# Squares of the second norm added on GpSimd, operations of GpSimd counted one by one, and more buffers for the value pages

## The reference

```python
sh1, sc1, g1, sh2, sc2, g2 = _modulation(c, w_mod, b_mod)
h = _rmsnorm(x, norm1_w) * (1 + sc1) + sh1
z = h @ w_in
rq, rk, rv, rg, mq, mk, mv = jnp.split(z, SPLITS, axis=-1)
ret_out, ret_s = _retention_branch(...)        # rotary on rq and rk, decayed scan in chunks of 128
moba_out = moba_mix(...)                       # prompt: causal; sample: top 3 blocks of the cache + own tokens
x = x + g1 * (jnp.concatenate([ret_out, moba_out], axis=-1) @ w_out)
h2 = _rmsnorm(x, norm2_w) * (1 + sc2) + sh2    # the second norm: mean of x*x over the 1024 features
x = x + g2 * ((jax.nn.silu(h2 @ w_gate) * (h2 @ w_up)) @ w_down)
```

## Time and profile before

| what | value |
|---|---|
| median of 3 runs | 1039.15 us (1037.05 to 1048.32) |
| the profiled execution | 1034.07 us, its span 1032.2 us |
| PE busy | 961.6 us, 93% |
| DVE busy | 624.5 us, 60% |
| ACT busy | 338.4 us, 33% |
| POOL busy | 139.4 us, 14% |
| chain that ended last | PE 72%, DVE 8%, DMA 7%, issue 5%, SP's queue 4%, DVE's queue 2% |
| bytes moved | 269.14 MB, mean 261 GB/s |

### The profile page before, as it was taken

How to read it: one execution, slowest core, us unless ns; L and a number is a source line. 1 busy time by engine, 2 the same in 40 slices (tenths; PEclk the granted TensorE clock), 3 DMA queues, 4 the chain that set the end, 5 groups by cost and what they waited for, 6 DMA issues and landing times.

```text
span 1032.2 us, 20974 instructions
## 1 busy us (share of the span) xinstructions
PE 961.6 (93%) x7919; PEld 675.8 (65%) x7919; DVE 624.5 (60%) x1067; ACT 338.4 (33%) x735; POOL 139.4 (14%) x129
## 2 busy tenths in 40 slices
PE   3879998999999987979989999999999999999996
PEld 2557775766666644547756767676777777777775
DVE  1566874677767667876788584432655555453244
ACT  5412233334333624542252152332333222121113
POOL 0011111444210132204151220000000000000000
PEclk9899999999999989999989899999999999999998
DMA  9978877999786889988998668778476988787652
GB/s 340 364 257 282 284 252 268 296 274 300 255 287 215 276 320 390 356 288 280 362 320 285 231 230 265 230 228 267 144 218 167 240 226 231 218 251 248 204 194 87
DMA packets 217973, 269.14 MB, mean 261 GB/s; under 512 B 13473, under 2 KB 168425, under 8 KB 209682
## 3 DMA queue, kind: packets, MB, share of 16 engines
q1 hardware_dynamic: 110226, 126.65, 38.7%
q10 hardware_dynamic: 98432, 74.04, 23.6%
q0 software_dynamic: 9216, 67.11, 17.7%
HBM read 260.04 MB, written 5.64 MB: 257 GB/s over the span
## 4 chain that ended last, share of the span: by engine, by line
PE 72%; DVE 8%; DMA 7%; issue 5%; SPq 4%; DVEq 2%; ACT 1%; POOLq 1%; POOL 1%; ACTq 0%
PE banks L1128 13%; PE banks L1129 12%; PE banks L1130 12%; PE banks L1078 6%; PE banks L1216 4%; PE banks L1141 4%; PE banks L1143 4%; PE banks L1142 4%; PE banks L1161 4%; DVE KT L1846 3%; DMA V<-in_cache_v 3%; DMA K<-in_cache_k,kidx 1%; SPq L420 1%; PE banks L1340 1%; DMA early<-in_w_mod 1%
## 5 line engine op out<-in xcount | busy, mean ns | idle before, releaser
L658 ACT ACTIVATE whi<-raw 128x1024 fp32r<-128x1024 f32 (+1 forms) x76 | 78.6, 1035 | 298.0 <-PE banks L1130 144.4
L1128 PE MATMUL banks<-ahi,whi 128*128 128x512 f32 x416 | 169.2, 407 | 0.1
L1846 DVE STREAM_TRANSPOSE KT<-K 128x2048 f32<-128x2048 f32 x63 | 145.5, 2310 | 30.0 <-DMA K<-in_cache_k,kidx 15.1
L1129 PE MATMUL banks<-alo,whi 128*128 128x512 f32 x416 | 163.5, 393 | 0.0
L1130 PE MATMUL banks<-ahi,rawlo 128*128 128x512 f32 x416 | 163.3, 393 | 0.0
L1809 DVE TENSOR_TENSOR rawlo<-raw,whi 128x1024 fp32r<-128x1024 f32 (+1 forms) x76 | 91.3, 1201 | 54.3 <-ACT whi L658 51.2
L523 POOL DMA_INDIRECT K<-in_cache_k,kidx x64 | 64.0, 1000 | 412.4 <-DVE KT L1846 363.7
L1128 PEld LDWEIGHTS banks<-ahi,whi 128*128 128x128 f32 x416 | 78.7, 189 | 31.2 <-issue 13.1
L1141 PE MATMUL banks<-ahi,whi 128*128 128x512 f32 x216 | 90.2, 417 | 1.2 <-DVE rawlo L1816 0.9
L1130 PEld LDWEIGHTS banks<-ahi,rawlo 128*128 128x128 f32 x416 | 78.8, 189 | 17.3
L1161 PE MATMUL banks<-KT,qbd 128*32 128x128 f32 x2048 | 74.0, 283 | 15.7 <-DVE KT L1846 13.0
(11 more groups left out here) (330 smaller groups left out, 1462.1 us busy)
## 6 DMA issues: line engine op xcount, KB each, us to landing
V<-in_cache_v SPq DMA_DIRECT2D x184, 256.0 KB
rawm<-in_w_mod ACTq DMA_DIRECT2D x14, 1024.0 KB
raw<-in_w_in ACTq DMA_DIRECT2D x12, 1024.0 KB
zT<-in_cache_v SPq DMA_DIRECT2D x48, 256.0 KB
raw<-in_w_gate ACTq DMA_DIRECT2D x22, 512.0 KB
raw<-in_w_up ACTq DMA_DIRECT2D x22, 512.0 KB
srw<-in_w_gate SPq DMA_DIRECT2D x22, 512.0 KB, 5.6
srw<-in_w_up SPq DMA_DIRECT2D x22, 512.0 KB, 7.3
```

The source lines that it names most:

```text
L658: act.activation(whi[t % 2][:, 0:kd, :], raw[u][:, 0:kd, t % 2 * P:(t % 2 + 1) * P], ACT.Copy).then_inc(s_hi, 1)
L1128: pe.matmul(out[:, :], whi[t % 2][:, k, :], hi(k), start=(first and n == 0), stop=False)
L1129: pe.matmul(out[:, :], whi[t % 2][:, k, :], lo(k), start=False, stop=False)
L1846: dve.transpose(KTb[:, :, :, :], Kb[g % 2][:, :]).then_inc(s_kt, 1)
```

## The change

1. Value groups 1 and 3 get four tiles of their own (`zT` from `RQ`, which the projection fills only later), so SP loads group 1 right behind group 0. Group 2 then waits for group 0's pages, group 4 for group 2's.
2. From group 17 to group 28 the values rotate through three rings in place of two (`raw[1]`, then `scr` and `free`, then `V`), with four more semaphores. Each group waits for the pages of the group three before it. ACT starts the first `w_out` chunk into `raw[1]` after group 26 in place of group 25.
3. The squares of the second norm: ACT writes the first into `rb`, and POOL adds those of k = 1 to 6 to it, one after each key gather from group 47 to group 52. PE sums `rb` and the last square alone, 2 sums in place of 8.
4. In `rotate` and `rotate_half` the drains go. Each operation raises `s_srot` or `s_rk`, and POOL waits for that count.

```diff
+RING_2 = {g: (1, 5)[(g - 17) % 3] for g in range(17, 28) if (g - 17) % 3 < 2}
+RING_FROM = min(RING_2)
+RING_2.update({1: 6, 3: 6})
+RING_2.update({g: 2 if g < 32 else 3 if g < 53 else 4 for g in range(29, NG, 2)})
+LANE = lambda g: 0 if g not in RING_2 else 2 if RING_2[g] == 5 else 1
...
     def values_before(g):
-        return max((x for x in range(g) if (x in RING_2) == (g in RING_2)), default=None)
+        return max((x for x in range(g) if LANE(x) == LANE(g)), default=None)
...
-            if g == 27:
+            if g == 18:
                 sp.wait_ge(s_md, NMOD)
...
-            pool.tensor_tensor(other, other, C("sin"), ALU.mult)
-            pool.tensor_tensor(z, z, C("cos"), ALU.mult)
-            pool.drain()
-            pool.tensor_tensor(z, z, other, ALU.add)
-            pool.drain().then_inc(s_rk, 1)
+            pool.tensor_tensor(other, other, C("sin"), ALU.mult).then_inc(s_srot, 1)
+            pool.tensor_tensor(z, z, C("cos"), ALU.mult).then_inc(s_srot, 1)
+            pool.wait_ge(s_srot, 2 * (m - M_TURN + 1))
+            pool.tensor_tensor(z, z, other, ALU.add).then_inc(s_rk, 1)
...
+        def add_squares(k):
+            pool.wait_ge(s_sqx, k + 1)
+            if k > 1:
+                pool.wait_ge(s_sqa, k - 1)
+            pool.tensor_tensor(rb[:, :], rb[:, :], stage[k % 2][:, :], ALU.add).then_inc(s_sqa, 1)
...
+            if 1 <= g - R_OUT - 3 < KT - 1:
+                add_squares(g - R_OUT - 3)
...
-                if f >= 3:
-                    act.wait_ge(s_ssm, f - 2)
-                act.activation(stage[(f - 1) % 2][:, :], x2T[:, f - 1, :], ACT.Square).then_inc(s_sqx, 1)
+                if f >= 4:
+                    act.wait_ge(s_sqa, f - 3)
+                act.activation(rb[:, :] if f == 1 else stage[(f - 1) % 2][:, :], x2T[:, f - 1, :], ACT.Square).then_inc(s_sqx, 1)
...
+        def sum_squares():
+            pe.matmul(DB[:, 0:TT], ident, C("pad0")[:, 0:TT], start=True, stop=False, skip_group_check=True)
+            pe.wait_ge(s_sqa, KT - 2)
+            sum_over_features(rb, False)
+            pe.wait_ge(s_sqx, KT)
+            sum_over_features(stage[1], True).then_inc(s_ssm, 1)
...
-            if f:
-                sum_squares(f - 1)
             if f == KT - 1:
                 turn_probs(B_NORM, 0)
-                sum_squares(KT - 1)
+                sum_squares()
```

More of the change, by code:

```diff
@@ L261, in decoder_step @@
              [at(B["K"] + ROWS * W + W * i, f"V{4 + i}", [P, W]) for i in range(4)],
-             [scr[:, 0, :], scr[:, 1, :], free[:, 0, :], free[:, 1, :]]]
+             [scr[:, 0, :], scr[:, 1, :], free[:, 0, :], free[:, 1, :]],
+             [zT[:, RQ + i, :] for i in range(4)]]
     ffa = at(ZT, "ffa", [P, 10, 2, T], F32R)
@@ L342, in decoder_step @@
     s_k = [sem(f"k_loaded{i}") for i in range(2)]
-    s_v = [sem(f"v_loaded{i}") for i in range(8)]
+    s_v = [sem(f"v_loaded{i}") for i in range(12)]
     s_kt, s_lg, s_own, s_s1 = sem("k_turned"), sem("logits"), sem("own_logits"), sem("block_sums")
@@ L384, in values @@
     def values(g):
-        if g in RING_2:
-            return rings[RING_2[g]], s_v[4:8], sum(x <= g for x in RING_2)
-        return rings[0], s_v[0:4], g + 1 - sum(x <= g for x in RING_2)
+        n = LANE(g)
+        return rings[RING_2.get(g, 0)], s_v[4 * n:4 * n + 4], sum(LANE(x) == n for x in range(g + 1))
     def values_before(g):
-        return max((x for x in range(g) if (x in RING_2) == (g in RING_2)), default=None)
+        return max((x for x in range(g) if LANE(x) == LANE(g)), default=None)
     def w_buffer(c):
@@ L451, in _ @@
         sp.wait_ge(s_lg, 9)
-        for s in range(4):
-            page(VB[s], s, s_v[s])
-        for g in range(1, M_TURN + 2 * HP - LAG + 2):
+        for g in range(M_TURN + 2 * HP - LAG + 2):
             m = g + LAG - 2
@@ L457, in _ @@
                 swap_halves(m)
+            bufs, sems, _ = values(g)
             for s in range(4):
-                sp.wait_ge(s_vd, g * 4 + s - 3)
-                page(VB[s], g * 4 + s, s_v[s])
-        with sp.Fori(M_TURN + 2 * HP - LAG + 2, min(RING_2)) as i:
+                if values_before(g) is not None:
+                    sp.wait_ge(s_vd, 4 * values_before(g) + s + 1)
+                page(bufs[s], 4 * g + s, sems[s])
+        with sp.Fori(M_TURN + 2 * HP - LAG + 2, RING_FROM) as i:
             for s in range(4):
@@ L464, in _ @@
                 page(VB[s], i * 4 + s, s_v[s])
-        for g in range(min(RING_2), NG):
+        for g in range(RING_FROM, NG):
             bufs, sems, _ = values(g)
@@ L531, in rotate_half @@
             o = (qrs, krs)[n][:, :].rearrange("p (h c d) -> p h c d", h=H, c=2)
-            pool.tensor_tensor(ta, z[:, :, half, :], cos, ALU.mult)
-            pool.tensor_tensor(tb, z[:, :, 1 - half, :], sin, ALU.mult)
-            pool.drain()
-            pool.tensor_tensor(o[:, :, half, :], ta, tb, op)
-            pool.drain()
+            done = 4 * HP + 3 * (2 * n + half)
+            pool.wait_ge(s_srot, done)
+            pool.tensor_tensor(ta, z[:, :, half, :], cos, ALU.mult).then_inc(s_srot, 1)
+            pool.tensor_tensor(tb, z[:, :, 1 - half, :], sin, ALU.mult).then_inc(s_srot, 1)
+            pool.wait_ge(s_srot, done + 2)
+            pool.tensor_tensor(o[:, :, half, :], ta, tb, op).then_inc(s_srot, 1)
         def masked_k(b):
@@ L723, in keep_z @@
             act.wait_ge(s_ft, m + 3)
+            if Z_OF[m] == RQ:
+                act.wait_ge(s_vd, 4 * 4)
             if Z_OF[m] in (RV, RV + 1):
@@ L874, in _ @@
             if hp == 3:
[L875 removed]
+                act.wait_ge(s_vd, 4 * 27)
                 next_chunk(0)
```

29 lines of the change are left out of this document (11 added, 18 removed).

## The result

| | before | changed |
|---|---|---|
| median of the runs | 1040.59 us (20 runs) | 1034.57 us (20 runs) |
| lowest to highest | 1034.26 to 1049.24 | 1031.14 to 1041.83 |
| the profiled execution | 1034.07 | 1035.24 (span 1033.4) |

The changed kernel takes 0.995 of the time of the kernel before, 95% interval 0.9929 to 0.997. That is 5.2 us less (3.1 to 7.4). The forecast was 11.5 us less. 1034.57 lies inside the wide range of the prediction (1018 to 1037) and outside the forecast's own (1023 to 1033). The two profiled executions don't show the gain, since the one of before was among the fastest of its kernel. So I compare them slot by slot. A slot's start is the first of its key matmuls in PE's timeline (L1161 before, L1180 after), and a slot's length runs to the next slot's start.

The account below looks back on a forecast made before the run. PE, busy 93% of the span, was taken as the bound, its stops as the target. Terms 3.9 + 2.8 + 4.6 + 0.2 = 11.5 us took 1039.15 to 1027.7 us; own range 1023 to 1033, wide range 1018 to 1037.

Parts of the forecast that it names:

- C: Second norm's squares: six PE sums of 0.87 us go, slot 49 loses some; 4.6 us gained if keys come in time.
- D: Drains in POOL's rotations replaced by counts: next key gather leaves 9 us earlier; 0.2 us gained, and C made whole.
- as long as ACT keeps pace: POOL's wait for a square ahead of the next gather costs nothing on this condition, each square being ready early enough.
- no 7.86 on POOL: Expected sign: the 7.86 us drain wait behind a gather in slot 45 disappears, the later gather leaving some 9 us earlier.
- a fallen clock: Sign of being wrong: granted clock falls in a stretch where PE now waits for DVE in one long piece.
- Term A: Slot 13, group 1's own buffer: its value stop goes, 4.94 us becoming 1.04; 3.9 us gained, from 1.3 to 3.9.
- Term B: Three rings in the retention: group 24's 3.7 us stop goes, DVE lets 2.8 us through; bounds 0 and 10.9.
- the third rival: Group 18's stop grows as group 1's shrinks, one more page 1.9 us; 1.2 us gained in all, 1038; chance 0.07.
- a change of this stop by more than 1 us: Sign of being wrong: group 18's stop in the retention, forecast to shorten by 0 to 0.8, changing either way.
- held-by-bytes rival: Bytes limit the retention, output-projection keys stay late: A whole, B zero, C and D 1.1; 5.0 us gained, 1034.2; chance 0.30.
- starved keys: Rival: key gathers land late, 12 slots losing 1.8 us each; net 10 us slower, 1049; chance 0.04.
- The rule on DVE and GpSimd: Two-input DVE instructions contend with GpSimd's SBUF reads: each add could hold DVE 1.28 us; sum 1.3 smaller, 1029 us.

Follow-up runs that it names:

- e3: Kernel before with only the squares added on POOL and counts in place of drains; rings and buffers as before: 1047.55 us, ratio 1.004.
- e5: Kernel before with only the squares added on POOL, all drains kept: 1044.26 us, ratio 1.0017.
- e6: Kernel before with only counts in place of drains, PE still summing the squares: 1040.33 us, ratio 0.9985.
- e4: Changed kernel with the retention state load moved from f = 2 to f = 4, behind the last w_out chunk: 1031.2 us, ratio 0.9884 to the kernel before.
- e8: Changed kernel with the retention state load moved from f = 2 to f = 6, behind all w_out chunks: 1028.08 us, ratio 0.986 to the kernel before.
- e9: Kernel before with only the retention state load moved from f = 2 to f = 6: 1038.81 us, ratio 0.9983.
- e10: Changed kernel without the squares part, PE summing each square as before: 1030.62 us, ratio 0.99 to the kernel before.
- e2: Kernel before with only the three rings for value groups 17 to 28: 1040.91 us, ratio 0.9983.
- e11: Changed kernel without the squares part and with the state load at f = 6: 1028.56 us, ratio 0.9886 to the kernel before.
- e7: Kernel before with squares on POOL, counts for drains and the state load at f = 6: 1042.02 us, ratio 1.0007.
- e12: Changed kernel with two rings in the retention as before and the state load at f = 6: 1030.98 us, ratio 0.9898 to the kernel before.

## Why the prediction was wrong, step by step

**The step that failed is terms C and D, in the sentence that D makes C whole and costs nothing as long as ACT keeps pace.** They were put at 4.8 us of gain and measured at 4.2 us of loss (e3). In the chain of keys the mechanism was right at every place named. The gather leaves 13 us earlier where 9 were forecast; no 7.86 on POOL; slots 43 to 47 are 4.5 us shorter. e5 shows what the prediction said of C without D. What it left out is the other transfer that a slot needs. Each slot takes 1 MB of keys, 1 MB of values and half a 1 MB chunk of w_out, 2.6 MB. At slot 47's 8.42 us in e6 that is 311 GB/s, at the 7.66 of the changed kernel 342, and the transfer engines gave 377, 313, 362, 401, 407 and 338 in the six stretches from 470 to 500. Those full stretches held the state load as well. The drain had been a throttle: it kept back gathers while the state load was under way and until just before the last chunk was issued (share 0.59 at 485 to 490 before, 1.03 now). I had asked who waits for the keys, and never who else uses the engines once the keys come early. ACT doesn't keep pace, since it waits for the chunk on its own queue.

The runs show three things about this. The chunk's lateness makes the stop, through ACT's split and DVE's part of it (the chain through the chunk, and slot 48 with the chunk's time in the table). Its place behind the state load matters: with that order changed the chunk comes 5 to 6 us sooner and the kernel is 7 to 9 us faster (e4, e8), while the same move gives the old kernel 1.8 (e9). And neither C nor D alone makes the stop in full: both together do (e5, e6, e10 against e3 and the changed kernel). That it takes both because a shorter slot asks more of full engines is the likeliest reading, from the numbers above, but no run varied the bytes of a slot at a fixed length, and none issued the chunk earlier or from another queue, so it is argued and not shown. Two readings limit it. Full engines alone don't make the chunk late: before, they were as full behind its issue (shares 1.05 and 1.02 from 490 to 500), and it took 8.5 us at most. And its place in the queue doesn't give the size: the state load landed 5.6 us ahead of the chunk's issue before, and 0.7 (e5), 2.2 (e10), 2.7 (e3) and 4.0 us (the changed kernel) behind it, and the chunk took 8.0, 11.3, 17.6 and 17.2 in these four. So 4.0 of the 17.2 us passed before the state load had landed, and what held the chunk for the other 13.2 stays open. The Trainium skill (DMA: Bandwidth & Descriptors, Queues, rings and completion order) says that each DMA engine goes round the queues that have work. By it ACT's queue keeps a third of the engines against SP's and the gathers', an estimated 7.7 us for 1 MB at a third of 407 GB/s, and the chunk shares that third with the state load while both are under way. The runs agree in kind, since the chunk took 10.9 us in e8 without the state load and 17.2 behind it in the changed kernel, but not in size: even the 10.9 is more than an equal third gives. No run here shows the shares of the queues by themselves.

**The price of the stop** was 6.95 us in slot 48 and 1.3 in slot 49 against the old profile, and by slot 54 the changed kernel was 1.5 us behind the old one's profile. Part of that price is the clock, 0.50 at 505 to 510. The prediction had a fallen clock among the things that would make it wrong, but with no place or price.

**Term A** (3.9, from 1.3 to 3.9) was right for the profiled execution: 24.69 to 20.81 is 3.9. Against the runs it was mis-sized: 8.5 (6.0 to 11.1) measured. Six other profiles without part A have a mean of 28.6 us in slots 13 and 14, so 7.7 are gained there. The term was taken from the one profile, and I carried the profile's 5 us under the median over unchanged, without asking in which places a slower execution is slower. This was one of them. No run shows a cost of the early megabyte, as forecast.

**Term B** (2.8, bounds 0 and 10.9) agrees with the 1.8 of e2, whose interval (-0.7 to 4.3) also holds no gain at all. In slots 29 to 42 the eight profiles with two rings have a mean of 98.4 us, the six with three rings 94.9, 3.5 less. Group 24 came on time as forecast. Group 18's stop, which I left as it was, grew instead: slot 30 went from a mean of 13.3 to 14.2, and in the pair of profiles shown by 1.9 us, as much as the third rival gave for one more page; that it is a page is not shown. The prediction had named a change of this stop by more than 1 us as a sign of being wrong. The wait of 1.90 for DVE at the end stayed.

**The squares themselves** (0.87 each): where nothing stops them, slots 43 to 47 go from 46.2 (mean of e6, e10, e11, with D) to 42.8, 3.4 us against the 4 x 0.87 = 3.5 of the prediction. Slot 49, hidden by the stop in the changed kernel, takes 8.27 in e7, e8 and e12 where it takes 8.65 in e6 and e10, 0.4 us less against the 0.3 of the prediction. Slot 48 is where the term failed: with the state load moved it takes 9.8 to 10.7 (e8, e12, e7) and not the 8.3 that 0.87 less than the 9.15 of e6 would be. D alone gave 1.6 where I had 0.2, with an interval from -0.8 to 4.0.

**The rivals.** That the measured 5.2 us lie at the 5.0 of the held-by-bytes rival is luck: its B was zero and its keys late, and in the runs the keys are early, and the measured B is 1.8, though with an interval that includes zero. The starved keys didn't happen either: in the changed kernel DVE waited for keys 6 times, 15.0 us in all, against 7 times and 15.1. The rule on DVE and GpSimd is taken up in the last part. Since A's surplus (4.6 us) hid half of the 9.0 by which C and D fell short, the total looked milder than the parts.

## What to carry to other kernels

When an edit lets one stream of transfers start earlier, list all streams that are in flight there, with their queues and their latest landing, and above all what stands ahead of the next needed transfer on its own queue. Here a load that nobody needed soon stood ahead of one that the path needed, and moving it was worth more than the edit. And look at a stop in more than one execution before you price it: here one profile had it at the full clock, and others of the same code there had it a little longer and followed by a lower clock, in five of six at about twice the price.
